# Splitting the last four weight chunks of a two-layer transformer kernel by token tile

## The chip, the cores and the metric

The kernel runs on one core of a Trainium2 chip. The metric is the device time of one launch, in microseconds. Three runs of the kernel before gave 2450.44, 2450.83 and 2454.04 us; the median is 2450.83 us. The engines are TensorE (PE, with PEld for its weight loads), VectorE (DVE), ScalarE (ACT), GpSimd (POOL) and SyncE (SP), whose queue issues nearly all the transfers.

## The reference

Two transformer layers run one after the other on 256 tokens of width 2048 in float32. What matters here is the end of the second one:

```
h = h + (silu(hn @ w_gate) * (hn @ w_up)) @ w_down      # w_down: 5632 x 2048
out = h * rsqrt(mean(h*h, axis=-1) + 1e-6) * final_norm  # one mean for each token
```

The mean is taken over all 2048 columns of a token, so no element of `out` can be scaled before the last column of the token's `h` is known. Two tokens never depend on each other in these two lines.

## The kernel before

Tokens lie on the 128 partitions, in two token tiles `t = 0, 1` (`NT`). Every large product is a list of groups, and each group yields 512 output columns (`CW`) for both tiles in two PSUM banks, `acc[g][0]` and `acc[g][1]`. The weights of a group come in chunks of 256 rows (`KC` = 2 times 128) by 512 columns, 512 KB each, through a ring of four slots (`RING`). SyncE loads a chunk into `w_raw` (L384), ACT rounds it to `w_hi` (L894), DVE forms the rest `w_lo` (L1206), and TensorE multiplies it (`columns`, L526 on). For each 128 rows and each tile there are three matmuls of 512 columns, high by high, high by low, low by high (L533 to L535), so 12 for a chunk. A slot is free for the next split when TensorE has used its chunk: each chunk's last matmul raises `w_used`, ACT waits on it for the chunk that comes four later, DVE waits for ACT, and TensorE for DVE (`w_split_lo`).

What each engine does beside this stream is listed by `plan()`: `put(n, step)` attaches a step to chunk `n`, and every engine runs its part of the steps between its chunks, in the order of the list. For each group of a down projection `residual` puts `res` (DVE adds the accumulators to the residual `x`, L1353), `square` (ACT squares the new columns and adds them up into `sumsq`, L1029), and in the second layer `times_gain` (DVE multiplies 512 columns of each tile by the final gain `fgain`, L1386) for the first three column groups. The second layer's down projection has four groups of 22 chunks. After the fourth comes `rstd`: DVE reduces the four partial sums of both tiles and adds epsilon (L1357, L1359), and POOL raises the result to the power -0.5 (L442).

Then the output is normalised. DVE takes columns 0 to 1023 and 1024 to 1535 of tile 0 (L1538) and columns 1536 to 2047 of both tiles, these with the gain (L1540); ACT takes columns 0 to 1535 of tile 1 in two parts (L1185). SyncE stores the output in four transfers of 128 x 1024 (L419), and waits for them.

Of the kernel before, what the change touches and what calls it, by code (L numbers as in the profile page):

```python
# [9 lines left out]
ALU = mybir.AluOpType  # L10
ACT = mybir.ActivationFunctionType
# [42 lines left out]
def plan():  # L54
# [10 lines left out]
    def put(n, *step):  # L65
        at.setdefault(n, []).append(step)
# [32 lines left out]
    def residual(n, g, b, gain):  # L99
        put(b, "res", g, n)  # L100
        put(b + 1, "square", g, n)
        if gain is not None:
            put(b + 1, "turn_x", n, g)
            put(b + 2, "split_x", n, gain, 0)
            put(b + 3, "split_x", n, gain, 1)
        elif n < 3:
            put(b + 3, "times_gain", n)
        if n == 3:
            put(b + (3 if gain is not None else 1), "rstd")


    for n in range(4):
# [80 lines left out]
        b = group("w_up_2", CW * j, CW, whole, "x")  # L193
    for n in range(4):
        b = group("w_down_2", CW * n, CW, list(range(FT // KC)), "f")
        residual(n, len(groups) - 1, b, None)
    return groups, first, at, up1, up2, b


# [19 lines left out]
def two_layer_kernel(nc, a, out):  # L219
# [6 lines left out]
    with ctx:  # L226
# [22 lines left out]
        hsum, hmean, hrstd = sb("hsum", [P, NT, 4]), sb("hmean", [P, NT, 4]), sb("hrstd", [P, NT, 4])  # L249
        lsum, lmean = sb("lsum", [P, 2, NT]), sb("lmean", [P, 2, NT])  # L250
        lrstd = sb("lrstd", [P, 2, NT])
        negmax, psum_, pinv = sb("negmax", [P, 4]), sb("p_sum", [P, 4]), sb("p_inv", [P, 4])

        with ExitStack() as r:
# [43 lines left out]
        pbuf = half_a.rearrange("p a b -> p (a b)")[:, 0:2 * KEYS]  # L298
        pT = half_b.rearrange("p a b -> p (a b)")[:, 0:2 * KEYS]
        rel = half_a.rearrange("p a b -> p (a b)")  # L300
        fgain = halves[:].rearrange("p s a b -> p (s a b)")

        acc = [[ctx.enter_context(nc.psum_tensor(f"acc{g}{t}", [P, CW], F32)) for t in range(NT)] for g in range(2)]
# [11 lines left out]
        gqk_ready, premultiplied, angles, tables = sem("gqk_ready"), sem("premultiplied"), sem("angles"), sem("tables")  # L315
# [9 lines left out]
        hidden, hidden_hi, f_ready = sem("hidden"), sem("hidden_hi"), sem("f_ready")  # L325
        dve_step, pool_step, normalised = sem("dve_step"), sem("pool_step"), sem("normalised")
        normalised_act = sem("normalised_act")

        block = ctx.enter_context(nc.Block())

# [30 lines left out]
        @block.sync  # L361
        def _(sp):
            chunk = Count()

            def load_x(n):

                sp.dma_start(x[:, :, n * CW:(n + 1) * CW],
                             a["x"][0].rearrange("(t p) d -> p t d", p=P)[:, :, n * CW:(n + 1) * CW]).then_inc(x_loaded[n], 16)

            def load(name, col, width, c):  # L370
                if chunk.now >= RING:

# [12 lines left out]
                chunk.now += 1  # L385

            def pair(j, wa, ca, wb, cb):
                for w, c0 in ((wa, ca), (wb, cb)):
                    for c in range(KT // KC):
                        load(w, j * CW + c0, CW, c)  # L390

            sp.dma_start(ident[:], a["c_ident"]).then_inc(ident_loaded, 16)
            sp.dma_start(rows[0:G_ROWS, 0:P], a["gains"]).then_inc(rows_loaded, 16)
            g = 0
            while g < len(groups):
                if g == G_UP1:
                    with_loop(sp, {"chunk": chunk}, lambda j: pair(j, "w_up", 0, "w_up", DFF), {"chunk": 16})
                    g += 2 * PAIRS
                elif g == G_UP2:
                    with_loop(sp, {"chunk": chunk}, lambda j: pair(j, "w_gate_2", 0, "w_up_2", 0), {"chunk": 16})  # L400
                    g += 2 * PAIRS
                else:
                    name, col, width, ks, _ = groups[g]
                    for c in ks:
                        if chunk.now < 4:
                            load_x(chunk.now)
                        load(name, col, width, c)
                        if name == "w_down_2" and col == 0 and c == 16:

                            sp.dma_start(fgain, a["final_norm_2"].rearrange("(a n) -> a n", a=1).to_broadcast([P, D]))\  # L410
                              .then_inc(fgain_loaded, 16)
                    g += 1

            for t, h, by_vector, by_scalar in ((0, 0, 1, 0), (1, 0, 0, 1), (0, 1, 3, 0), (1, 1, 4, 2)):
                if by_vector:
                    sp.wait_ge(normalised, by_vector)
                if by_scalar:
                    sp.wait_ge(normalised_act, by_scalar)
                sp.dma_start(out[0, t * P:(t + 1) * P, h * 2 * CW:(h + 1) * 2 * CW],  # L419
                             x[:, t, h * 2 * CW:(h + 1) * 2 * CW]).then_inc(stored, 16)  # L420
            sp.wait_ge(stored, 16 * 2 * NT)

        @block.gpsimd
        def _(pool):
# [77 lines left out]
            for n in range(n_end + 8):  # L502
                for step_, *args in at.get(n, []):
                    if step_ == "isc" and args[0] == 5:

                        pool.wait_ge(rel_full, 6)
                        pool.dma_start(pool_w[:], a["pool_w"].rearrange("w (k p) d -> p w k d", p=P)).then_inc(pool_loaded, 16)
                    if step_ in mine:
                        mine[step_](*args)

        @block.tensor
        def _(pe):
# [13 lines left out]
            def columns(c, k, width, operand, start, stop, g):  # L526

                hi, lo = operand
                slot = chunk.now % RING
                for t in range(NT):  # L530
                    o = acc[g][t][:, 0:width]
                    l, m = hi[:, t * P:(t + 1) * P], lo[:, t * P:(t + 1) * P]
                    pe.matmul(o, l, w_hi[:, slot, k, 0:width], start=start, stop=False)  # L533
                    pe.matmul(o, l, w_lo[:, slot, k, 0:width], start=False, stop=False)  # L534
                    last = pe.matmul(o, m, w_hi[:, slot, k, 0:width], start=False, stop=stop)  # L535
                return last

            def kw_columns(c, g):
# [342 lines left out]
        def _(act):  # L881
# [296 lines left out]
                g += 1  # L1178
            for n in range(n_end - LEAD, n_end + 8):
                run(n)  # L1180
            act.wait_ge(rstd_ready, 5)
            act.wait_ge(premultiplied, 6)
            for lo_, hi_ in ((0, 2 * CW), (2 * CW, 3 * CW)):
                v = x[:, 1, lo_:hi_]
                act.activation(v, v, ACT.Copy, scale=rstd[:, 1:2]).then_inc(normalised_act, 1)  # L1185

        @block.vector
        def _(dve):
# [191 lines left out]
            def on_times_gain(n):  # L1380

                dve.wait_ge(squared, n_squared[0] + 2 * (n + 1))
                dve.wait_ge(fgain_loaded, 16)
                for t in range(NT):
                    v = x[:, t, n * CW:(n + 1) * CW]
                    dve.tensor_tensor(v, v, fgain[:, n * CW:(n + 1) * CW], ALU.mult).then_inc(premultiplied, 1)  # L1386

            def on_rstd():
                n_squared[0] += 8
# [34 lines left out]
            def run(n):  # L1424
                for step_, *args in at.get(n, []):
                    if step_ in mine:
                        mine[step_](*args)

            dve.memset(minus_half[:], -0.5).then_inc(consts_set, 1)
            dve.wait_ge(cols_ready, 1)  # L1430
            for m in range(KT // 2):
# [98 lines left out]
                run(n)  # L1530


            dve.wait_ge(rstd_ready, 5)
            dve.wait_ge(premultiplied, 6)
            for t, lo_, hi_ in ((0, 0, 2 * CW), (0, 2 * CW, 3 * CW), (0, 3 * CW, D), (1, 3 * CW, D)):
                v, r = x[:, t, lo_:hi_], rstd[:, t:t + 1]
                if hi_ < D:
                    dve.tensor_scalar(v, v, r, None, ALU.mult).then_inc(normalised, 1)  # L1538
                else:
                    dve.scalar_tensor_tensor(v, v, r, fgain[:, lo_:hi_], ALU.mult, ALU.mult).then_inc(normalised, 1)  # L1540


_WHOLE = ["x", "w_in", "pool_w", "w_out", "w_up", "w_down", "positions_2", "final_norm_2"]
# [38 lines left out]
```

## Time and profile before

| | us |
|---|---|
| median of 3 runs | 2450.83 |
| lowest, highest run | 2450.44, 2454.04 |
| span of the profiled execution | 2451.8 |
| PE busy | 2431.2 (99% of the span) |
| DVE busy | 1319.7 (54%) |
| ACT busy | 1181.0 (48%) |
| POOL busy | 55.8 (2%) |

For the profiled execution the page gives its span, from the first instruction to the last, and no time of its own beyond that. The span lies 1.0 us above the median of the three runs and inside their spread. PE is busy nearly all the time, and its granted clock is full over all 40 slices; only the last microseconds of the span have no matmul in them.

### The profile page before, as it was taken

The numbers are of one execution on the slowest core, as the hardware profiler recorded it, in microseconds if no ns is written. First come the engines' busy times: TensorE is split into PE (matmuls) and PEld (weight loads), VectorE is DVE, ScalarE is ACT, GpSimd is POOL, SyncE is SP. The second block draws the span as 40 slices with busy tenths as digits, with TensorE's granted clock in tenths as the row PEclk, the third lists the DMA queues.
The fourth block names the chain that finished last, engine by engine and source line by source line (L and its number), as shares of the span: only waits on it lengthen the run. The fifth ranks groups of instructions, "written<-read, shape, count | busy, mean of one in ns | idle before, by whom it ended". The sixth has DMA issues, their size and how long they took to land.

```text
span 2451.8 us, 29803 instructions
## 1 busy us (share of the span) xinstructions
PE 2431.2 (99%) x11143; PEld 2016.1 (82%) x11143; DVE 1319.7 (54%) x1478; ACT 1181.0 (48%) x1488; POOL 55.8 (2%) x96
## 2 busy tenths in 40 slices
PE   8999999999999999999999999999999999999998
PEld 7788888888888888888888888888888888888886
DVE  4675455666666655445454454565545445454443
ACT  5544455555555544445455544544444444444443
POOL 0000000000000000001120000000000000000000
PEclk9999999999999999999999999999999999999999
DMA  6565455555555555556655555555665666655653
GB/s 229 171 189 164 146 182 188 186 183 187 186 184 184 188 185 188 189 189 186 185 170 172 159 161 186 185 185 184 188 190 187 190 192 187 190 189 205 191 192 142
DMA packets 240899, 449.38 MB, mean 183 GB/s; under 512 B 20027, under 2 KB 26747, under 8 KB 240683
## 3 DMA queue, kind: packets, MB, share of 16 engines
q1 hardware_dynamic: 239904, 445.94, 57.4%
q0 software_dynamic: 544, 2.06, 0.3%
q8 instruction: 59, 0.97, 0.2%
q14 instruction: 29, 0.24, 0.0%
q10 hardware_dynamic: 363, 0.18, 0.0%
HBM read 446.02 MB, written 2.10 MB: 183 GB/s over the span
## 4 chain that ended last, share of the span: by engine, by line
PE 69%; issue 29%; DVE 0%; DMA 0%; ACT 0%; SPq 0%; POOLq 0%; POOL 0%; DVEq 0%; ACTq 0%
PE acc L533 22%; PE acc L535 22%; PE acc L534 21%; PE bank L524 2%; PE bank L665 1%; PE bank L693 0%; PE bank L723 0%; PE bank L642 0%; DMA x_res<-in_x 0%; PE bank L694 0%; PE bank L668 0%; DVE xT_lo L1321 0%; DVE w_lo L1206 0%; PE bank L708 0%; PE acc L545 0%
## 5 line engine op out<-in xcount | busy, mean ns | idle before, releaser
L1206 DVE TENSOR_TENSOR w_lo<-w_raw,w_hi 128x1024 fp32r<-128x1024 f32 (+1 forms) x844 | 1031.2, 1222 | 1084.5 <-ACT w_hi L894 1082.7
L894 ACT ACTIVATE w_hi<-w_raw 128x1024 fp32r<-128x1024 f32 (+1 forms) x844 | 891.1, 1056 | 1222.7 <-PE acc L535 1220.0
L533 PE MATMUL acc<-w_hi,xT_hi 128*128 128x512 f32 (+1 forms) x2240 | 881.1, 393 | 1.2 <-DVE w_lo L1206 1.2
L535 PE MATMUL acc<-w_hi,xT_lo 128*128 128x512 f32 (+1 forms) x2240 | 871.1, 389 | 0.0
L534 PE MATMUL acc<-w_lo,xT_hi 128*128 128x512 f32 (+1 forms) x2240 | 870.2, 388 | 0.0
L535 PEld LDWEIGHTS acc<-w_hi,xT_lo 128*128 128x128 f32 x2240 | 421.0, 188 | 87.6
L533 PEld LDWEIGHTS acc<-w_hi,xT_hi 128*128 128x128 f32 x2240 | 421.1, 188 | 87.3 <-issue 3.3
L534 PEld LDWEIGHTS acc<-w_lo,xT_hi 128*128 128x128 f32 x2240 | 421.4, 188 | 83.7
L533 PE MATMUL acc<-w_hi,f_hi 128*128 128x512 f32 x704 | 277.2, 394 | 0.0
L535 PE MATMUL acc<-w_hi,f_lo 128*128 128x512 f32 x704 | 276.1, 392 | 0.0
L534 PE MATMUL acc<-w_lo,f_hi 128*128 128x512 f32 x704 | 273.6, 389 | 0.0
L535 PEld LDWEIGHTS acc<-w_hi,f_lo 128*128 128x128 f32 x704 | 132.2, 188 | 30.3
L534 PEld LDWEIGHTS acc<-w_lo,f_hi 128*128 128x128 f32 x704 | 132.2, 188 | 29.5
L533 PEld LDWEIGHTS acc<-w_hi,f_hi 128*128 128x128 f32 x704 | 132.3, 188 | 26.6
L533 PE MATMUL acc<-w_hi,y_hi 128*128 128x512 f32 x256 | 101.1, 395 | 0.0
L535 PE MATMUL acc<-w_hi,y_lo 128*128 128x512 f32 x256 | 100.2, 391 | 0.0
L534 PE MATMUL acc<-w_lo,y_hi 128*128 128x512 f32 x256 | 100.1, 391 | 0.0
L1446 DVE SCALAR_TENSOR_TENSOR halves<-bank,cols,halves 128x254 f32<-128x254 f32 (+1 forms) x176 | 76.5, 476 | 5.9
L524 PE MATMUL bank<-ident,stage 128*128 128x128 f32 (+1 forms) x435 | 57.0, 272 | 4.4 <-DMA stage<-in_gains 4.4
L524 PEld LDWEIGHTS bank<-ident,stage 128*128 128x128 f32 (+1 forms) x435 | 50.9, 140 | 11.8 <-DMA stage<-in_gains 4.4
L535 PEld LDWEIGHTS acc<-w_hi,y_lo 128*128 128x128 f32 x256 | 48.1, 188 | 10.7
L534 PEld LDWEIGHTS acc<-w_lo,y_hi 128*128 128x128 f32 x256 | 48.1, 188 | 10.2
(189 smaller groups left out, 1162.9 us busy)
## 6 DMA issues: line engine op xcount, KB each, us to landing
w_raw<-in_w_up SPq DMA_DIRECT2D x264, 512.0 KB, 3.4
w_raw<-in_w_in SPq DMA_DIRECT2D x200, 512.0 KB, 3.6
w_raw<-in_w_down SPq DMA_DIRECT2D x176, 512.0 KB, 3.7
w_raw<-in_w_gate SPq DMA_DIRECT2D x88, 512.0 KB, 3.5
w_raw<-in_w_out SPq DMA_DIRECT2D x64, 512.0 KB, 3.6
w_raw<-in_w_branch_a SPq DMA_DIRECT2D x16, 512.0 KB, 3.5
w_raw<-in_w_branch_b SPq DMA_DIRECT2D x16, 512.0 KB, 3.6
w_raw<-in_w_in SPq DMA_DIRECT2D x10, 320.0 KB, 3.1
```

Of the source, the lines that this page charges most:

```text
L524: return pe.transpose(T[bank][:, pos:pos + part], src, ident[0:part, 0:part])
L533: pe.matmul(o, l, w_hi[:, slot, k, 0:width], start=start, stop=False)
L534: pe.matmul(o, l, w_lo[:, slot, k, 0:width], start=False, stop=False)
L535: last = pe.matmul(o, m, w_hi[:, slot, k, 0:width], start=False, stop=stop)
L665: last = pe.matmul(o, q[:, blk * P:(blk + 1) * P], k[:, 0:nk], start=True, stop=which != "mla")
L894: act.activation(in_slot(w_hi, slot, width), in_slot(w_raw, slot, width), ACT.Copy).then_inc(w_split_hi, 1)
L1206: dve.tensor_tensor(in_slot(w_lo, slot, width), in_slot(w_raw, slot, width), in_slot(w_hi, slot, width).bitcast(F32), ALU.subtract).then_i ...
L1446: last = dve.scalar_tensor_tensor(o, T[bank][:, cc * S:(cc + 1) * S - back], cols[:, bass.ds(j * 4 + k, 1)], o, ALU.mult, ALU.add)
```

## The change

TensorE goes through all but the last four chunks of the last group as before. Then it takes these four chunks for tile 0 alone (24 matmuls into `acc[..][0]`, `first_tile_done`), and after that the same four chunks for tile 1 (24 matmuls into `acc[..][1]`), raising `w_used` once for each chunk in this second pass. The steps `res`, `square` and `rstd` of the fourth column group leave the plan. In their place each tile has a sequence of its own at the end: DVE adds the accumulator to the residual in a separate buffer `last`, ACT squares and sums, POOL takes the power, DVE and ACT scale, and the tile is stored.

The sum over the first three column groups, with epsilon, is made earlier (`sum_before`), its square root (POOL) is put beside the 512 new columns as a 513th, and ACT's square-and-sum over 513 elements gives the whole sum in one instruction. The division by 2048 moves into the gain, which is multiplied once by sqrt(2048) in the step of the first column group. ACT's squares go to `spare` in SBUF, not to a PSUM bank. DVE normalises columns 0 to 1023 and 1536 to 2047 of each tile, ACT 1024 to 1535. Tile 0 is stored in two halves of 1024 columns by SyncE; tile 1 in columns 0 to 1023 and 1536 to 2047 by SyncE and 1024 to 1535 by ACT's own queue.

```diff
@@ plan @@
     for n in range(4):
         b = group("w_down_2", CW * n, CW, list(range(FT // KC)), "f")
-        residual(n, len(groups) - 1, b, None)
+        if n < 3:
+            residual(n, len(groups) - 1, b, None)
@@ sync @@
-            for t, h, by_vector, by_scalar in ((0, 0, 1, 0), (1, 0, 0, 1), (0, 1, 3, 0), (1, 1, 4, 2)):
...
+            sp.wait_ge(normalised, 1)
+            store(0, 0, 2 * CW)
+            sp.wait_ge(normalised, 2)
+            sp.wait_ge(normalised_act, 1)
+            store(0, 2 * CW, D)
+            sp.wait_ge(normalised, 3)
+            store(1, 0, 2 * CW)
+            sp.wait_ge(normalised, 4)
+            store(1, 3 * CW, D)
+            sp.wait_ge(stored, 16 * 5)
@@ gpsimd @@
+            pool.wait_ge(before_ready, 1)
+            for t in range(NT):
+                pool.tensor_tensor(last[:, t, CW:CW + 1], sum_before[:, t:t + 1], plus_half[:], ALU.pow).then_inc(root_ready, 1)
+            for t in range(NT):
+                pool.wait_ge(last_squared, t + 1)
+                pool.tensor_tensor(last_r[:, t:t + 1], sumsq[:, t, 3:4], minus_half[:, 0:1], ALU.pow).then_inc(last_rstd, 1)
@@ tensor @@
+            def last_columns(t, c, par, ends):
+
+                slot = (chunk.now + c) % RING
+                kt = (FT // KC - RING + c) * KC
+                for k in range(KC):
+                    h, l = f_hi[:, kt + k, t * P:(t + 1) * P], f_lo[:, kt + k, t * P:(t + 1) * P]
+                    pe.matmul(acc[par][t][:], h, w_hi[:, slot, k], start=False, stop=False)
+                    pe.matmul(acc[par][t][:], h, w_lo[:, slot, k], start=False, stop=False)
+                    last = pe.matmul(acc[par][t][:], l, w_hi[:, slot, k], start=False, stop=ends and k == KC - 1)
+                return last
...
-                for c, kc in enumerate(ks):
+                in_turn = ks[:-RING] if g == len(groups) - 1 else ks
+                for c, kc in enumerate(in_turn):
...
+                if g == len(groups) - 1:
+                    for c in range(RING):
+                        pe.wait_ge(w_split_lo, chunk.value(c + 1))
+                        last = last_columns(0, c, group.now % 2, c == RING - 1)
+                    last.then_inc(first_tile_done, 1)
+                    for c in range(RING):
+                        last_columns(1, c, group.now % 2, c == RING - 1).then_inc(w_used, 1)
+                    chunk.now += RING
@@ scalar @@
-            for lo_, hi_ in ((0, 2 * CW), (2 * CW, 3 * CW)):
-                v = x[:, 1, lo_:hi_]
-                act.activation(v, v, ACT.Copy, scale=rstd[:, 1:2]).then_inc(normalised_act, 1)
+            act.wait_ge(root_ready, 2)
+            for t in range(NT):
+                act.wait_ge(last_added, t + 1)
+                act.activation(spare[:, t, 0:CW + 1], last[:, t, 0:CW + 1], ACT.Square, accum_out=sumsq[:, t, 3:4]).then_inc(last_squared, 1)
+                act.wait_ge(last_rstd, t + 1)
+                v = x[:, t, 2 * CW:3 * CW]
+                act.activation(v, v, ACT.Copy, scale=last_r[:, t:t + 1]).then_inc(normalised_act, 1)
+            act.wait_ge(normalised_act, 2)
+            act.dma_start(out[0, P:2 * P, 2 * CW:3 * CW], x[:, 1, 2 * CW:3 * CW]).then_inc(stored, 16)
@@ vector @@
-                dve.wait_ge(fgain_loaded, 16)
+                if n == 0:
+                    dve.wait_ge(fgain_loaded, 16)
+                    link(dve.tensor_scalar(fgain, fgain, D ** 0.5, None, ALU.mult))
+                    linked()
...
+                if n == 2:
+                    link(dve.tensor_reduce(sum_before[:], sumsq[:, :, 0:3], AX.X, ALU.add))
+                    linked()
+                    dve.tensor_scalar(sum_before[:], sum_before[:], D * EPS, None, ALU.add).then_inc(before_ready, 1)
...
+            dve.memset(plus_half[:], 0.5)
...
-            for t, lo_, hi_ in ((0, 0, 2 * CW), (0, 2 * CW, 3 * CW), (0, 3 * CW, D), (1, 3 * CW, D)):
...
+            for t in range(NT):
+                if t == 0:
+                    dve.wait_ge(first_tile_done, 1)
                 else:
+                    finished(g_last)
+                v = x[:, t, 3 * CW:D]
+                dve.tensor_tensor(last[:, t, 0:CW], acc_last[t][:], v, ALU.add).then_inc(last_added, 1)
+                dve.wait_ge(last_added, t + 1)
+                link(dve.tensor_tensor(v, last[:, t, 0:CW], fgain[:, 3 * CW:D], ALU.mult))
+                dve.wait_ge(last_rstd, t + 1)
+                linked()
+                r = last_r[:, t:t + 1]
+                dve.tensor_scalar(x[:, t, 0:2 * CW], x[:, t, 0:2 * CW], r, None, ALU.mult).then_inc(normalised, 1)
+                dve.tensor_scalar(v, v, r, None, ALU.mult).then_inc(normalised, 1)
```

## Rows read from the trace of the kernel before

**Rows 1.** The page: span, busy time of the engines, and the chain's shares.
```profile
span 2451.8 us, 29803 instructions
...
PE 2431.2 (99%) x11143; PEld 2016.1 (82%) x11143; DVE 1319.7 (54%) x1478; ACT 1181.0 (48%) x1488; POOL 55.8 (2%) x96
...
PE 69%; issue 29%; DVE 0%; DMA 0%; ACT 0%; SPq 0%; POOLq 0%; POOL 0%; DVEq 0%; ACTq 0%
```

**Rows 2.** Timeline of PE at the last 49 matmuls: start, duration, what (us).
```profile
2429.41 0.39 PE L533 MATMUL acc<-w_hi,f_hi 128*128 128x512 f32 x1
2429.64 0.39 PE L534 MATMUL acc<-w_lo,f_hi 128*128 128x512 f32 x1
...
2439.94 0.39 PE L534 MATMUL acc<-w_lo,f_hi 128*128 128x512 f32 x1
2440.17 0.40 PE L535 MATMUL acc<-w_hi,f_lo 128*128 128x512 f32 x1
```

**Rows 3.** Timeline of ACT and DVE: the split of the last chunk.
```profile
2429.67 1.06 ACT L894 ACTIVATE w_hi<-w_raw 128x1024 fp32r<-128x1024 f32 x1 [1.69 <-PE acc L535]
...
2430.76 1.23 DVE L1206 TENSOR_TENSOR w_lo<-w_raw,w_hi 128x1024 fp32r<-128x1024 f32 x1 [1.52 <-ACT w_hi L894]
```

**Rows 4.** Timeline of DVE, ACT and POOL from the last matmul to the power.
```profile
2440.60 1.29 DVE L1353 TENSOR_TENSOR x_res<-acc,x_res 128x512 f32<-128x512 f32 x2 [8.62 <-PE acc L535]
...
2441.33 0.60 ACT L1029 ACTIVATE bank<-x_res 128x512 f32<-128x512 f32 x1 [10.60 <-DVE x_res L1353]
2441.86 0.18 ACT L1029 ACTIVATION_READ_ACCUMULATOR bank<-x_res 128x1 f32 x1
...
2442.68 0.19 ACT L1029 ACTIVATION_READ_ACCUMULATOR bank<-x_res 128x1 f32 x1
2442.90 0.16 DVE L1357 TENSOR_REDUCE meansq<-sumsq 128x2 f32<-128x8 f32 x1 [1.00 <-ACT bank L1029]
2443.09 0.17 DVE L1359 TENSOR_SCALAR meansq<-meansq 128x2 f32<-128x2 f32 x1
2443.34 0.70 POOL L442 TENSOR_TENSOR rstd<-meansq,minus_half 128x2 f32<-128x2 f32 x1 [720.77 <-DVE meansq L1359]
```

**Rows 5.** Timeline of DVE, ACT and SP: normalisation and stores.
```profile
2444.07 1.15 DVE L1538 TENSOR_SCALAR x_res<-x_res,rstd 128x1024 f32<-128x1024 f32 x2 [0.81 <-POOL rstd L442]
2444.85 0.36 SPq L419 DMA_DIRECT2D out<-x_res  x1
...
2445.80 0.74 DVE L1540 SCALAR_TENSOR_TENSOR x_res<-x_res,rstd,halves 128x512 f32<-128x512 f32 x1
```

**Rows 6.** Groups by line and shape on the residual: count, min/median/max in ns.
```profile
L1029 ACT ACTIVATE halves<-x_res x32: 612/631/642, 25.0 to 1713.8; 128x512 f32<-128x512 f32 x32
...
L1353 DVE TENSOR_TENSOR x_res<-acc,x_res x32: 680/682/692, 305.9 to 2441.2; 128x512 f32<-128x512 f32 x32
...
L1386 DVE TENSOR_TENSOR x_res<-x_res,halves x6: 682/684/687, 2269.8 to 2391.3; 128x512 f32<-128x512 f32 x6
...
L419 SPq DMA_DIRECT2D out<-x_res x4: 364/526/1108, 2444.9 to 2446.6; - x4
L1185 ACT ACTIVATE x_res<-x_res,rstd x2: 705/926/1147, 2444.1 to 2445.1; 128x1024 f32<-128x1024 f32 x1, 128x512 f32<-128x512 f32 x1
L1538 DVE TENSOR_SCALAR x_res<-x_res,rstd x2: 481/616/752, 2444.1 to 2444.7; 128x1024 f32<-128x1024 f32 x1, 128x512 f32<-128x512 f32 x1
```

**Rows 7.** POOL's powers by line and shape: count, busy us, mean ns, idle before.
```profile
L448 POOL TENSOR_TENSOR hrstd<-hmean,minus_half 128x8 f32<-128x8 f32 x4 | 10.2, 2548 | 145.5 <-DVE hmean L1234 145.5
...
L442 POOL TENSOR_TENSOR rstd<-meansq,minus_half 128x2 f32<-128x2 f32 x5 | 3.6, 712 | 2065.8 <-DVE meansq L1359 2065.7
...
L459 POOL TENSOR_TENSOR lrstd<-lmean,minus_half 128x2 f32<-128x2 f32 x2 | 1.9, 954 | 18.7 <-DVE lmean L1396 18.7
```

**Rows 8.** Transfers from 2440 to 2453: GB/s in 40 slices of 0.325 us.
```profile
GB/s 0 0 0 0 0 0 0 0 0 25 0 0 25 0 0 0 0 189 403 391 416 391 416 391 403 403 416 391 416 391 416 429 391 202 0 0 0 0 0 0
```

**Rows 9.** The line of the stores: time from issue to landing.
```profile
DMA to landing us min/median/max: 2.7/3.9/4.8
```

**Rows 10.** Transfers from 2350 to 2440: packets and rate; then the queue's share.
```profile
DMA packets 7407, 14.31 MB, mean 159 GB/s; under 512 B 440, under 2 KB 440, under 8 KB 7404
...
q1 hardware_dynamic: 7404, 14.26, 46.5%
```

**Rows 11.** Timeline of DVE around the first `times_gain`.
```profile
2269.85 1.29 DVE L1386 TENSOR_TENSOR x_res<-x_res,halves 128x512 f32<-128x512 f32 x2
2271.46 1.23 DVE L1206 TENSOR_TENSOR w_lo<-w_raw,w_hi 128x1024 fp32r<-128x1024 f32 x1 [0.32 <-ACT w_hi L894]
```

More of the change, by code:

```diff
@@ L105, in residual @@
             put(b + 3, "split_x", n, gain, 1)
-        elif n < 3:
+        else:
             put(b + 3, "times_gain", n)
         if n == 3:
-            put(b + (3 if gain is not None else 1), "rstd")
+            put(b + 3, "rstd")
     for n in range(4):
@@ L251, in two_layer_kernel @@
         lrstd = sb("lrstd", [P, 2, NT])
+        sum_before, last_r, plus_half = sb("sum_before", [P, NT]), sb("last_r", [P, NT]), sb("plus_half", [P, 1])
         negmax, psum_, pinv = sb("negmax", [P, 4]), sb("p_sum", [P, 4]), sb("p_inv", [P, 4])
@@ L300, in two_layer_kernel @@
         rel = half_a.rearrange("p a b -> p (a b)")
+        last = stage[:].rearrange("p g t c -> p g (t c)")
+        spare = w_raw[:].rearrange("p r k n -> p r (k n)")
         fgain = halves[:].rearrange("p s a b -> p (s a b)")
@@ L314, in two_layer_kernel @@
         kw_turned, kw_scaled = sem("kw_turned"), sem("kw_scaled")
-        gqk_ready, premultiplied, angles, tables = sem("gqk_ready"), sem("premultiplied"), sem("angles"), sem("tables")
+        gqk_ready, angles, tables = sem("gqk_ready"), sem("angles"), sem("tables")
         consts_set, squared, mean_ready, rstd_ready = sem("consts_set"), sem("squared"), sem("mean_ready"), sem("rstd_ready")
@@ L327, in two_layer_kernel @@
         normalised_act = sem("normalised_act")
+        first_tile_done, last_added, last_squared, last_rstd, before_ready, root_ready = (sem(n) for n in (
+            "first_tile_done", "last_added", "last_squared", "last_rstd", "before_ready", "root_ready"))
         block = ctx.enter_context(nc.Block())
@@ L412, in _, with store @@
                     g += 1
-            for t, h, by_vector, by_scalar in ((0, 0, 1, 0), (1, 0, 0, 1), (0, 1, 3, 0), (1, 1, 4, 2)):
[L415 to L421, printed above, removed]
+            def store(t, lo_, hi_):
+                sp.dma_start(out[0, t * P:(t + 1) * P, lo_:hi_], x[:, t, lo_:hi_]).then_inc(stored, 16)
+            sp.wait_ge(normalised, 1)
[8 more added lines that the diff above has]
+            sp.wait_ge(stored, 16 * 5)
         @block.gpsimd
@@ L1180, in _ @@
                 run(n)
-            act.wait_ge(rstd_ready, 5)
-            act.wait_ge(premultiplied, 6)
-            for lo_, hi_ in ((0, 2 * CW), (2 * CW, 3 * CW)):
-                v = x[:, 1, lo_:hi_]
-                act.activation(v, v, ACT.Copy, scale=rstd[:, 1:2]).then_inc(normalised_act, 1)
+            act.wait_ge(root_ready, 2)
[7 more added lines that the diff above has]
+            act.dma_start(out[0, P:2 * P, 2 * CW:3 * CW], x[:, 1, 2 * CW:3 * CW]).then_inc(stored, 16)
         @block.vector
@@ L1382, in on_times_gain @@
                 dve.wait_ge(squared, n_squared[0] + 2 * (n + 1))
-                dve.wait_ge(fgain_loaded, 16)
+                if n == 0:
+                    dve.wait_ge(fgain_loaded, 16)
+                    link(dve.tensor_scalar(fgain, fgain, D ** 0.5, None, ALU.mult))
+                    linked()
                 for t in range(NT):
                     v = x[:, t, n * CW:(n + 1) * CW]
-                    dve.tensor_tensor(v, v, fgain[:, n * CW:(n + 1) * CW], ALU.mult).then_inc(premultiplied, 1)
+                    link(dve.tensor_tensor(v, v, fgain[:, n * CW:(n + 1) * CW], ALU.mult))
+                if n == 2:
+                    link(dve.tensor_reduce(sum_before[:], sumsq[:, :, 0:3], AX.X, ALU.add))
+                    linked()
+                    dve.tensor_scalar(sum_before[:], sum_before[:], D * EPS, None, ALU.add).then_inc(before_ready, 1)
             def on_rstd():
@@ L1530, in _ @@
                 run(n)
-            dve.wait_ge(rstd_ready, 5)
-            dve.wait_ge(premultiplied, 6)
-            for t, lo_, hi_ in ((0, 0, 2 * CW), (0, 2 * CW, 3 * CW), (0, 3 * CW, D), (1, 3 * CW, D)):
-                v, r = x[:, t, lo_:hi_], rstd[:, t:t + 1]
-                if hi_ < D:
-                    dve.tensor_scalar(v, v, r, None, ALU.mult).then_inc(normalised, 1)
-                else:
-                    dve.scalar_tensor_tensor(v, v, r, fgain[:, lo_:hi_], ALU.mult, ALU.mult).then_inc(normalised, 1)
+            g_last = len(groups) - 1
+            acc_last = acc[g_last % 2]
+            for t in range(NT):
+                if t == 0:
+                    dve.wait_ge(first_tile_done, 1)
+                else:
+                    finished(g_last)
[8 more added lines that the diff above has]
+                dve.tensor_scalar(v, v, r, None, ALU.mult).then_inc(normalised, 1)
 _WHOLE = ["x", "w_in", "pool_w", "w_out", "w_up", "w_down", "positions_2", "final_norm_2"]
```

## The prediction

> **What bounds the kernel now.** I read the page first. PE is busy for 2431.2 of 2451.8 us and the chain that ended last is matmuls and their issue; the other engines are busy half the time or less [rows 1]. So nearly all the time is matmuls, one after the other, and the change removes none. The timeline of PE at the end shows their pace: starts at 2429.41 and 2440.17 with 47 steps between them, 10.76 / 47 = 0.229 us for one matmul of 512 columns, 2.75 us for a chunk of 12 [rows 2]. The last one ends at 2440.57, and 2451.8 - 2440.57 = 11.2 us have no matmul. Only this tail can change, so I followed the end engine by engine.
>
> The tail has two parts with different limits. In the first, one engine waits for another. DVE adds tile 0 and tile 1 (from 2440.60), ACT squares both (last read ends at 2442.68 + 0.19), DVE reduces and adds epsilon (to 2443.26), POOL takes the power (2443.34 to 2444.04) [rows 4]; the first 1024 columns are scaled from 2444.07 on, and SyncE issues the first store at 2444.85 [rows 5]. In the second part the transfers rule. The rate stands near 403 GB/s from the middle of slice 18 to the middle of slice 34, each 0.325 us long, so from 2445.7 to 2450.9: 5.2 us, and 4 x 524,288 bytes / 5.2 us = 403 GB/s [rows 8]. The last data are ready at 2445.80 + 0.74 = 2446.54 [rows 5], long before. So the end is set by the start of the first store and by the bytes that follow it, not by the normalisation that ends last. From the last packet to the end of the span it is 0.9 us.
>
> **The change, part by part.**
>
> *Matmuls.* Their number stays (48 for the last four chunks), and tile 1's last should still end at 2440.57. The first of the 48 starts at 2429.41; tile 0's 24th starts 23 x 0.229 later, at 2434.68, and ends at 2435.08 [rows 2]. The order costs nothing if the weights are ready. The pass over tile 0 takes the chunks at twice the pace: the fourth is wanted at its 19th matmul, 2429.41 + 18 x 0.229 = 2433.5. Its split waits for the chunk ahead of these four to be used, as before: ACT from 2429.67, DVE from 2430.76 to 2431.99 [rows 3], 1.5 us ahead. The third is wanted at 2432.2 and split a chunk earlier than the fourth, at 2429.2. Cost 0; if this cover were gone, all lateness would come through. That the four slots are released later is waited for by nothing, since no load follows.
>
> 24 matmuls in a row into one bank don't stand in the trace; three in a row do, and the step inside such a three is the same 0.23 us as the mean over all [rows 2]. I bound the cost from 0 to rival B and take 0, the end that the pace inside the threes is nearest to.
>
> *Tile 0's own end*, from 2435.1: add 0.68, to 2435.8 [rows 6]; square and read 0.72, to 2436.6 [rows 4]; POOL 0.41 (below) with hops, to 2437.1; DVE 0.75 + 0.48, to 2438.4, with ACT's 0.71 beside it [rows 6]. Its stores are issued at 2437.9 and 2438.4, start moving 0.85 us later (before: 2444.85 to 2445.7 [rows 5, 8]), and take 2.6 us for 1 MB: out by 2441.4. All of it lies beside tile 1's matmuls, and DVE is free 2.2 us before it is wanted at 2440.60. Cost 0; 1 MB of stores leaves the tail.
>
> *Tile 1's own end.* Add from 2440.60. ACT started at 2441.33 on the first add alone, and so it will now, to 2441.86 + 0.18 = 2442.04 [rows 4]. Its squares go to SBUF: 0.631 us there against 0.602, 0.03 more [rows 4, 6]; a 513th column is 1/512 of that. DVE's product with the gain (0.68 [rows 6]) runs beside ACT, over by 2442.0. POOL starts 0.08 us after its input, as it did behind DVE [rows 4]. Its power took 2.548 us over 8 columns and 0.712 over 2 [rows 7], so (2.548 - 0.712) / 6 = 0.31 a column and 0.10 fixed, an estimate of 0.41 for one column. Bounds: 0.41, and the 0.95 of the slower two-column power [rows 7]; I take 0.41. So POOL ends at 2442.55, DVE scales 1024 columns in 0.75 [rows 6] from 2442.58 to 2443.33, and the store is issued at 2443.35 against 2444.85: 1.5 us earlier. Of this 0.83 is the second square (between the ends of the two reads), 0.39 the reduction and epsilon (2442.87 to 2443.26) [rows 4], 0.3 POOL.
>
> ACT's 512 columns are done at 2442.58 + 0.71 = 2443.3 and are issued on its own queue; DVE's last 512 at 2443.33 + 0.48 = 2443.8 [rows 6]. SyncE's first issue takes 0.36 us [rows 5], so the second isn't held up. An issue by ACT behind data isn't in the rows; by SyncE's four it costs 0.36 to 1.11 us [rows 6], and at either the packets are queued before the first 512 KB are out. Cost 0.
>
> *The stores.* Packets start at 2443.35 + 0.85 = 2444.2. The 1,048,576 bytes in the tail need 2.6 us at 403 GB/s [rows 8]. Half of them now have rows of 2 KB in place of 4 KB. The weight loads have 2 KB rows: 159 GB/s at a share of 46.5% is 342 GB/s at full share [rows 10], 1.5 us for the half against 1.3. So 2.6 to 2.8 us, I take 2.7: last packet at 2446.9 and, with the same 0.9 us behind it, the end at 2447.8. It was 2451.8: **4.0 us less**, 1.5 from the chain and 2.5 from the transfers. Bounds: 4.1 with the faster rate; 3.6 with the slower rate for all bytes (3.1 us), and 3.1 with the slower power too.
>
> Does the last store alone end later than the backlog? The first of before landed in 2.7 us with 1.3 of moving [rows 9], so 1.4 are fixed; 256 KB issued at 2443.8 would land at 2443.8 + 1.4 + 0.65 = 2445.9. The backlog is later.
>
> The stores of this trace ran at 403 GB/s for 5 us [rows 8]. The Trainium skill ("DMA: Bandwidth & Descriptors", Specifications) gives about 358 GB/s as one core's limit to HBM. By it the 1 MB would take 2.9 us and the saving would be 3.8; the trace disagrees, and the measurement decides.
>
> *Earlier edits.* Scaling the gain adds one DVE instruction over 2048 columns. From 0.481 us for 512 and 0.752 for 1024 [rows 6] each further 512 costs 0.27, so about 1.3 us. It stands ahead of a split that started at 2271.46; the products before it ended at 2271.14 [rows 11], now at about 2272.5, so this split comes 1.1 us late. A split ends 2.3 us after ACT starts it [rows 3], and the ring gives it three chunks, 8.2 us: 5.8 us of slack hide it. The reduction and addition into `sum_before` (0.16 + 0.17 [rows 4]) are hidden likewise, two root instructions run on an idle POOL, and the new memset stands ahead of waits for the first transfers. Cost 0; without cover 1.3 + 0.4 us.
>
> **The sum.** The span goes from 2451.8 to 2447.8. The median of before is 1.0 us below its profiled span; I take the 4.0 off the median: 2450.8 - 4.0 = **2446.8 us**, 0.16% less. A measurement of this kernel tells 0.2%, 4.9 us, from no change, so this counts as no change unless it reaches 2445.9.
>
> **The rivals.**
>
> *A: the transfers stop being the limit.* If the stores of two queues drain faster than those of one, the last landing sets the end: 2445.9 + 0.4 = 2446.3, which is 5.5 less, 2445.3 us. For it: the last store waits for nothing else. Against: one queue already kept the rate steady near 403 GB/s, slice after slice [rows 8]. With the scatter of medians added, 16% that the time passes the 4.9 us.
>
> *B: one bank for 24 matmuls is slower.* If a matmul into the same bank had to see the one before it finish, the pace would be its 0.39 us instead of 0.229 [rows 2], 48 x 0.16 = 7.7 us more, less 4.0: +3.7, 2454.5 us, slower than before. The step at which it decides is 4.0 / 48 = 0.08 us a matmul; with 0.19 more it passes 2455.7. Against it: the pace inside the present threes. 4%.
>
> *C: a handover is late.* DVE comes late to tile 1 if tile 0's end takes over 5.5 us; the split's 1.5 us are used up; or POOL's power on one column is no shorter than 0.95. Each costs 0.5 to 3 us: 2447.3 to 2449.8. For it: five hops a tile, and POOL's spans are rough. Against it: 1.5 to 2.2 us of room in the first two. 13%.
>
> *D: it doesn't do what it says*: the four stores still bunch at the end, 2450.8 us. Tile 0's would have to come 5 us late for that. 2%.
>
> **How the numbers follow.** The forecast with a saving of 3.1 to 4.8: 65%; A 16, B 4, C 13, D 2. The medians scatter by about 1 us (two runs 0.4 apart, one at 2454.04). The range takes the forecast with that scatter, A down to 2445.1 and most of C: 2445.1 to 2449.5. Faster than 2445.9: 16%; slower than 2455.7: 3%, B at its worst or a disturbed median; 81% within.
>
> **What would show it.** In the profile after: PE keeps 0.229 us through the last 48 with no wait for `w_lo`; DVE's adds start near 2435.1 and 2440.6; POOL's last power takes 0.41 us and ends near 2442.55; tile 1's first store is issued near 2443.35; the rate line shows two humps of 2.7 us, the first over by 2441.5, the second from 2444.2 to 2446.9; span near 2447.8. It is wrong if PE shows gaps in the last 11 us, if tile 0's stores reach into the tail, or if the last hump is much longer than 2.8 us.

## The result

The changed kernel takes 2463.24 us (median of 5 runs, 2461.76 to 2464.69) against 2451.48 (5 runs, 2450.44 to 2454.04): the ratio is 1.0047, 95% interval 1.0036 to 1.0058. It is 11.8 us slower. The forecast was 2446.8, 4 us faster, within 2445.1 to 2449.5, with a chance of 3% for slower by more than 0.2%: the direction is wrong and the time is far outside the range.

The page of the changed kernel, span and busy time:

```profile
span 2462.2 us, 29808 instructions
...
PE 2445.3 (99%) x11143; PEld 2016.1 (82%) x11143; DVE 1321.7 (54%) x1482; ACT 1181.0 (48%) x1488; POOL 57.8 (2%) x99
```

Against [rows 1] the span grew by 10.4 us and PE's busy time by 14.1, with the same 11143 matmuls. So PE lost 14.1 us and 3.7 were gained elsewhere. The busy times of DVE, ACT and POOL changed by 2.0 us or less.

**Where the 14 us are.** The timeline of PE, one row at each end of 24 matmuls (8 rows of this line apart); the columns are start and modelled duration. First products of `x` (up projection, near 700 us), then of `f` (last down projection). The kernel before:

```profile
699.76 0.39 PE L533 MATMUL acc<-w_hi,xT_hi 128*128 128x512 f32 x1
...
705.20 0.39 PE L533 MATMUL acc<-w_hi,xT_hi 128*128 128x512 f32 x1
...
2299.63 0.39 PE L533 MATMUL acc<-w_hi,f_hi 128*128 128x512 f32 x1
...
2305.12 0.39 PE L533 MATMUL acc<-w_hi,f_hi 128*128 128x512 f32 x1
```

The changed kernel:

```profile
700.00 0.39 PE L551 MATMUL acc<-w_hi,xT_hi 128*128 128x512 f32 x1
...
705.44 0.39 PE L551 MATMUL acc<-w_hi,xT_hi 128*128 128x512 f32 x1
...
2299.75 0.40 PE L551 MATMUL acc<-w_hi,f_hi 128*128 128x512 f32 x1
...
2305.35 0.40 PE L551 MATMUL acc<-w_hi,f_hi 128*128 128x512 f32 x1
```

The step, the time from one matmul's start to the next one's, is the difference of two such rows divided by 24. `x` steps at 5.44 / 24 = 0.2267 us in both. `f` stepped at 5.49 / 24 = 0.2288 and now steps at 5.60 / 24 = 0.2333. The same holds at 300 us, in products of `y`, and at 1650, in those of `m_hl`: places whose instructions the change doesn't touch. 3384 matmuls have a stationary operand other than `x` (2112 `f`, 768 `y`, 384 `m_hl`, 120 latents); 3384 x 0.0045 = 15 us, the 14.1 of the page. The granted clock is 1.00 in both.

What `y`, `m_hl`, the latents and `f` have in common, and `x` has not, is their place in SBUF. The change allocates three small tensors (`sum_before`, `last_r`, `plus_half`) behind `minus_half` and the other small ones. Counted as 32 bytes a partition each, they move all that is allocated later by 96 bytes. `x` and the weights' buffers are allocated earlier and stay.

**The tail** did nearly as forecast. ACT, DVE, POOL and the queues of the changed kernel at tile 1's end, in that order:

```profile
2455.38 0.63 ACT L1222 ACTIVATE w_raw<-stage 128x513 f32<-128x513 f32 x1 [3.44 <-DVE stage L1591]
2455.91 0.19 ACT L1222 ACTIVATION_READ_ACCUMULATOR w_raw<-stage 128x1 f32 x1
...
2457.51 0.39 ACTq L1227 DMA_DIRECT2D out<-x_res  x1
```

```profile
2449.05 0.69 DVE L1591 TENSOR_TENSOR stage<-acc,x_res 128x512 f32<-128x512 f32 x1 [3.22 <-PE acc L564]
...
2454.65 0.69 DVE L1591 TENSOR_TENSOR stage<-acc,x_res 128x512 f32<-128x512 f32 x1 [2.29 <-PE acc L564]
...
2456.76 0.75 DVE L1597 TENSOR_SCALAR x_res<-x_res,last_r 128x1024 f32<-128x1024 f32 x1 [0.69 <-POOL last_r L527]
```

```profile
2456.18 0.54 POOL L527 TENSOR_TENSOR last_r<-sumsq,minus_half 128x1 f32<-128x1 f32 x1 [5.00 <-ACT w_raw L1222]
```

```profile
2457.54 0.81 SPq L422 DMA_DIRECT2D out<-x_res  x2
```

The last matmul ends at 2454.62 (2454.22 + 0.40). From there to the end of the span it is 7.6 us; it was 11.2 [rows 1, 2]. SyncE issues tile 1's first store 2.92 us after the last matmul, where it was 4.28 [rows 5]. DVE was free for tile 1 in time: it waited 2.29 us for tile 1's last matmul.

The transfers of the changed kernel from 2450 to 2462.2, GB/s in 40 slices of 0.305 us:

```profile
GB/s 0 0 0 27 0 27 0 0 0 295 416 349 430 416 416 389 403 322 0 0 0 0 0 0 0 0 0 255 416 389 369 383 423 349 383 389 81 0 0 0
```

There are two humps in place of the one of [rows 8]. Tile 0's ends at 2455.4; tile 1's lasts from 2458.4 to 2461.0, 2.7 us in place of 5.2.

### The profile page after: what moved, and what is told of

It reads as the page before. It is cut to its first block, busy times and chain, and to the rows that moved or that the text cites. A ratio compares the mean times of both kernels' runs of the same rounds, so it can differ in the third digit from the quotient of the medians.

```text
span 2462.2 us, 29808 instructions
## 1 busy us (share of the span) xinstructions
PE 2445.3 (99%) x11143; PEld 2016.1 (82%) x11143; DVE 1321.7 (54%) x1482; ACT 1181.0 (48%) x1488; POOL 57.8 (2%) x99
## 4 chain that ended last, share of the span: by engine, by line
PE 99%; DVE 0%; DMA 0%; issue 0%; ACT 0%; SPq 0%; POOLq 0%; POOL 0%; DVEq 0%; ACTq 0%
PE acc L551 31%; PE acc L553 31%; PE acc L552 31%; PE bank L542 3%; PE bank L703 1%; PE bank L731 0%; PE bank L761 0%; PE bank L680 0%; DMA x_res<-in_x 0%; PE bank L732 0%; PE bank L706 0%; PE bank L746 0%; DVE xT_lo L1363 0%; DVE w_lo L1248 0%; PE acc L564 0%
```

## The experiments

Places below are byte offsets in a partition, counted through the kernel's allocations in their order, each start on a multiple of 32. No trace shows an address. What speaks for the count is that experiments three and six, 64 bytes added before the change and 96 + 224 after it, come to the same distance by it and have the same step, where 16 bytes off cost the step in nearly every group of experiment ten. "Distance" is the start of the stationary operand less the start of the weights' buffer it is multiplied with, modulo 256 (the parts used later lie at multiples of 512 from these starts). I began with another idea, that a start on a multiple of 64 is what counts; two experiments overturned it and its successor.

### One: the changed kernel, 32 bytes of padding

```diff
-negmax, psum_, pinv = sb("negmax", [P, 4]), sb("p_sum", [P, 4]), sb("p_inv", [P, 4])
+negmax, psum_, pinv = sb("negmax", [P, 4]), sb("p_sum", [P, 4]), sb("p_inv", [P, 4]); sb("pad", [P, 8])
```

> The changed kernel with one unused tensor of 32 bytes a partition behind the small tensors, ahead of y_hi; nothing else differs. The three new small tensors take 96 bytes there, so that all large tensors behind them (y_hi, y_lo, m_hl, f_hi, f_lo, cqT) begin at 32 past a multiple of 64, where before they began on one. Theory P (position): the matmuls whose stationary operand lies there step at 0.2333 us in place of 0.2288, which is the loss; with the pad the step is 0.2288 again in all groups, PE busy falls from 2445.3 to about 2431, and the time is that of before less the shorter tail (11.2 us before, 7.6 in the changed kernel): 2451.5 - 3.6 = 2447.9 us. Theory C (code): another layout of the instructions or the added semaphores slow PE; the pad changes nothing and the time stays at 2463.

Measured: 2462.86 us (ratio 1.0048, 1.0034 to 1.0062), `f` at 0.2333. A multiple of 64 doesn't do it. By this run alone theory C stood as well.

### Two: the kernel before, 32 bytes

```diff
+; sb("pad", [P, 8])
```

> The kernel before with the same unused 32 bytes, and no other edit. Theory P: y, m and f products step at 0.2333 us, PE busy rises by about 14 us, time 2451.5 + 14 = 2465.5 us, with not one instruction changed. Theory C: nothing moves, 2451.5.

Measured: 2466.2 us (1.0062, 1.0048 to 1.0076). Its page, and `f` in the timeline of PE:

```profile
span 2464.4 us, 29803 instructions
...
PE 2445.1 (99%) x11143; PEld 2014.5 (82%) x11143; DVE 1319.5 (54%) x1478; ACT 1181.8 (48%) x1488; POOL 55.7 (2%) x96
```

```profile
2299.71 0.39 PE L533 MATMUL acc<-w_hi,f_hi 128*128 128x512 f32 x1
...
2305.31 0.39 PE L533 MATMUL acc<-w_hi,f_hi 128*128 128x512 f32 x1
```

PE's busy time rises by 13.9 us with not one instruction changed (29803 in both). An unused tensor is enough for the whole loss. That the change's instructions add nothing to it is shown by experiment six.

### Three: the kernel before, 64 bytes

```diff
+; sb("pad", [P, 16])
```

> The kernel before with 64 unused bytes: the large tensors move but begin again on a multiple of 64 (now of 128 too). Theory P in the form that only the place within 64 bytes counts: 2451.5 us, same steps. Rival: any shift against the weights' buffers slows it (then about 2465), or a multiple of 128 is better still (then under 2449, with a step below 0.2288 in the y, m and f products).

Measured: 2445.67 us (0.9975, 0.9965 to 0.9986), 6 us faster than the kernel before. The rival was right that there is something better:

```profile
span 2443.5 us, 29803 instructions
...
PE 2423.9 (99%) x11143; PEld 2017.1 (83%) x11143; DVE 1319.5 (54%) x1478; ACT 1180.9 (48%) x1488; POOL 55.7 (2%) x96
```

```profile
2300.17 0.39 PE L533 MATMUL acc<-w_hi,f_hi 128*128 128x512 f32 x1
...
2305.61 0.39 PE L533 MATMUL acc<-w_hi,f_hi 128*128 128x512 f32 x1
```

`f` is at 5.44 / 24 = 0.2267, as `x` is in all kernels up to here. The kernel before was itself at a middle level.

### Four: the old order of the last four chunks

In the kernel of experiment one:

```diff
                     for c in range(RING):
                         pe.wait_ge(w_split_lo, chunk.value(c + 1))
                         last = last_columns(0, c, group.now % 2, c == RING - 1)
-                    last.then_inc(first_tile_done, 1)
-                    for c in range(RING):
+                        if c == RING - 1:
+                            last.then_inc(first_tile_done, 1)
                         last_columns(1, c, group.now % 2, c == RING - 1).then_inc(w_used, 1)
```

> The changed kernel with the pad of 32 bytes and the last four chunks in the old order: each chunk for tile 0, then for tile 1; the two tiles' ends keep their new sequences, tile 0's starting when its last matmul is done, now 6 matmuls (1.4 us) before the end in place of 24 (5.5 us). If the order by tiles is what takes 1 MB of stores out of the tail: tile 0's stores are issued about 2.8 us after its last matmul, so some 1.4 us behind PE's end, DVE comes to tile 1 only after tile 0's scaling, at about PE's end + 2.1 us, and the span ends 2.5 to 3.5 us later than the padded kernel: 2450.5 to 2451.5 us. Rival: the gain of the tail is all from the shorter chain (one square, no reduction), and the order is worth under 1 us: 2448.0 to 2449.0.

Measured: 2465.84 us against 2462.86 of experiment one on the same chip, 3.0 us more; the runs of the two just overlap (2464.60 to 2465.92 against 2462.37 to 2465.21). (The absolute times were expected with the padding's gain, which didn't come; the difference is what counts.) In the profiled executions the tail is 9.4 us against 7.6. DVE comes to tile 1 late:

```profile
2454.20 0.75 DVE L1597 TENSOR_SCALAR x_res<-x_res,last_r 128x1024 f32<-128x1024 f32 x1 [0.74 <-POOL last_r L527]
2454.87 0.48 DVE L1598 TENSOR_SCALAR x_res<-x_res,last_r 128x512 f32<-128x512 f32 x1
2455.27 0.68 DVE L1591 TENSOR_TENSOR stage<-acc,x_res 128x512 f32<-128x512 f32 x1
```

The last matmul ended at 2453.41, DVE adds tile 1 at 2455.27. So the order by tiles is worth 2 to 3 us, and it costs PE nothing: both kernels step at 0.2333 in this group, two passes or one.

### Five and six: the changed kernel, 96 and 224 bytes

```diff
+; sb("pad", [P, 24])      # experiment six: [P, 56]
```

> The changed kernel with 96 unused bytes ahead of y_hi, so that y, m and f begin on a multiple of 128 (of 256 too, 0 within 512 bytes counted as 256). So far the step of the products was: 0.2267 us where the stationary operand began at 128 within 512 (x in all kernels; y, m, f in the padded kernel before), 0.2288 at 64, 0.2333 at 96, 160 and 192. Theory M128 (a multiple of 128 is what counts): 0.2267 in all groups, PE busy about 2424, time 2445.7 less the 3.6 us of the shorter tail: 2442 us, faster than both. Theory M256 or relative (only the same place within 256 or 512 bytes as the weights' buffer, which is at 128): step 0.2288 or 0.2333, 2447.9 to 2462.

> The changed kernel with 224 unused bytes: y, m, f begin at 384 within 512 bytes, 128 within 256. M128: as with 96 bytes, 2442 us. M256: 0.2267 here and not there. Only the same place within 512 as before (128): slow in both.

Measured: 2459.9 us (1.0033, 1.0022 to 1.0043) with 96 and **2440.98 us** (0.9955, 0.9938 to 0.9972) with 224. The page and PE's timeline with 224:

```profile
span 2438.8 us, 29808 instructions
...
PE 2423.0 (99%) x11143; PEld 2015.3 (83%) x11143; DVE 1322.0 (54%) x1482; ACT 1180.6 (48%) x1488; POOL 58.2 (2%) x99
```

```profile
2299.82 0.39 PE L551 MATMUL acc<-w_hi,f_hi 128*128 128x512 f32 x1
...
2305.26 0.39 PE L551 MATMUL acc<-w_hi,f_hi 128*128 128x512 f32 x1
```

A multiple of 128 isn't enough (96 bytes: 0.2325), the same place within 256 is (0.2267). PE's busy time is 2423.0 us, against 2423.9 in experiment three, which has the old instructions at the same distance: the change's instructions, the two passes among them, cost PE nothing. The changed kernel so placed beats the kernel before by 10.7 us and experiment three by 4.7. What is left open is whether the place counts by itself or against the weights' buffers.

### Seven and eight: moving x, moving the weights' buffers

```diff
 # seven
-xT_hi, xT_lo = sb("xT_hi", ...), sb("xT_lo", ...)
+sb("pad_a", [P, 8]); xT_hi, xT_lo = sb("xT_hi", ...), sb("xT_lo", ...); sb("pad_b", [P, 8])
 # eight
-w_hi, w_lo = sb("w_hi", ...), sb("w_lo", ...)
+sb("pad_a", [P, 8]); w_hi, w_lo = sb("w_hi", ...), sb("w_lo", ...); sb("pad_b", [P, 8])
```

> The kernel before with 32 unused bytes ahead of xT_hi and 32 behind xT_lo: x begins at 160 within 512 bytes, the weights' buffers at 192, y, m and f at 128. If only the stationary operand's own place counts: x products (6720 matmuls) step at 0.2333 for 0.2267, 44 us more; the other 3384 at 0.2267 for 0.2288, 7 us less; 2451.5 + 37 = 2489 us. If its place relative to the weights' buffer counts: x at -32 is slow (+44), y, m, f at -64 stay at 0.2288, as in the kernel before (also -64): 2496 us. If the weights' own place counts, the y, m and f products go to 0.2333: 2511 us.

> The kernel before with 32 unused bytes ahead of w_hi and 32 behind w_lo: w_hi and w_lo begin at 160 within 512 bytes, x, y, m and f at 128. If only the stationary operand's place counts: all products at 0.2267, 2445.7 us (as the kernel before with 64 bytes). If the moving operand's place counts, alone or relative to the stationary one (now -32): all products at about 0.2333, 10104 matmuls x 0.0066 = 67 us over 2445.7: 2512 us.

Measured: seven 2491.9 us (1.0161, 1.0135 to 1.0187), eight 2506.6 us (1.0222, 1.0195 to 1.0248). The total of seven doesn't decide, 2489 and 2496 are both near; the steps do. PE's timeline in seven, `x` then `f`:

```profile
700.17 0.39 PE L533 MATMUL acc<-w_hi,xT_hi 128*128 128x512 f32 x1
...
705.77 0.39 PE L533 MATMUL acc<-w_hi,xT_hi 128*128 128x512 f32 x1
...
2299.81 0.39 PE L533 MATMUL acc<-w_hi,f_hi 128*128 128x512 f32 x1
...
2305.30 0.39 PE L533 MATMUL acc<-w_hi,f_hi 128*128 128x512 f32 x1
```

`x` is at 0.2333 now. `f` begins at 128 within 256, the place that gave 0.2267 in three and six, but steps at 0.2288 here, since the buffers moved by 64: the distance is -64, as in the kernel before. In eight only the buffers are moved, and the products of `x`, `y`, `m_hl` and `f` all step at 0.2333. PE's busy time in eight:

```profile
PE 2485.3 (99%) x11143; PEld 2013.0 (80%) x11143; DVE 1319.4 (53%) x1478; ACT 1182.1 (47%) x1488; POOL 54.6 (2%) x96
```

### Nine: everything off by 32

```diff
+sb("pad_a", [P, 8])  # ahead of xT_hi; and sb("pad_b", [P, 16]) ahead of y_hi
```

> The kernel before with 32 unused bytes ahead of xT_hi, so that every large tensor moves by 32, and 64 more ahead of y_hi. x, the weights' buffers, y, m and f then all begin at 160 within 512 bytes: none on a multiple of 64, and all at distance 0 from each other within 256. Theory R (the distance of the stationary operand from the weights' buffers, counted within 256 bytes, sets the step: 0 gives 0.2267 us, -64 0.2288, -32, +32, +64 and +128 0.2325 to 0.2334): every product at 0.2267, 2445.7 us, as the kernel before with 64 bytes. Theory A (the place of either operand by itself counts): all products at 0.233, about 2507 to 2512 us.

Measured: 2444.7 us (0.9971, 0.9960 to 0.9983), within the intervals the same as experiment three. PE's busy time and timeline:

```profile
PE 2423.3 (99%) x11143; PEld 2015.0 (82%) x11143; DVE 1319.6 (54%) x1478; ACT 1181.0 (48%) x1488; POOL 55.7 (2%) x96
```

```profile
2300.09 0.39 PE L533 MATMUL acc<-w_hi,f_hi 128*128 128x512 f32 x1
...
2305.53 0.39 PE L533 MATMUL acc<-w_hi,f_hi 128*128 128x512 f32 x1
```

By the count no large tensor begins on a multiple of 64, and all products have the fast step. Against experiment three a shift of everything by 32 changed nothing, and a shift of the buffers alone by 32 cost 62 us: it is the distance between stationary operand and weights' buffer that counts, not the place of either.

### Ten: two more distances

```diff
+; sb("pad", [P, 16])               # as in experiment three
+sb("pad_y", [P, 40], F32, r)      # ahead of y_hi
-f_hi, f_lo = sb("f_hi", [P, FT, S], F32R, r), sb("f_lo", [P, FT, S], F32R, r)
+f_raw = sb("f_raw", [P, 2 * FT * S + 4], F32R, r)
+f_hi = f_raw[:, 4:4 + FT * S].rearrange("p (a b) -> p a b", b=S)
+f_lo = f_raw[:, 4 + FT * S:4 + 2 * FT * S].rearrange("p (a b) -> p a b", b=S)
```

> The kernel before with 64 unused bytes (all distances 0), and then f moved by 16 bytes and y, m and the latents by 160. It measures two further distances of theory R: f at +16 (2112 matmuls), y, m and latents at +160 (1272), x still at 0. If any distance other than 0 and -64 costs the full step of 0.2333: 3384 x 0.0066 = 22 us over 2445.7, 2468 us. If 16 bytes are too little to matter, f stays at 0.2267 and the time is about 2454. If +160 = -96 is between, y and m at 0.229 to 0.233.

Measured: 2464.76 us (1.0054, 1.0039 to 1.0070). `f`, 16 bytes off, steps at 0.2333 in seven of its eight groups, and so do `y` and `m_hl` at +160. So 16 bytes can cost the full step. But the third group of the first down projection, from 995 to 1056 us, has the fast step from end to end. PE's timeline in the first group, then in the third:

```profile
890.15 0.39 PE L536 MATMUL acc<-w_hi,f_raw 128*128 128x512 f32 x1
...
895.75 0.39 PE L536 MATMUL acc<-w_hi,f_raw 128*128 128x512 f32 x1
...
1010.64 0.39 PE L536 MATMUL acc<-w_hi,f_raw 128*128 128x512 f32 x1
...
1016.08 0.39 PE L536 MATMUL acc<-w_hi,f_raw 128*128 128x512 f32 x1
```

That is 5.60 / 24 = 0.2333 and 5.44 / 24 = 0.2267. The two groups have the same `f`, and by the kernel's counters the same ring slots and the same PSUM banks. So where the distance isn't 0, the addresses alone don't fix the step; what else does isn't known.

### Eleven: tile 0's stores held back

In the kernel of experiment six:

```diff
-            sp.wait_ge(normalised, 1)
+            sp.wait_ge(normalised, 3)
             store(0, 0, 2 * CW)
```

> The changed kernel with 224 unused bytes (2441.0 us), and SyncE waiting for tile 1's first normalised columns before it issues tile 0's stores: all 2 MB of stores lie in the tail again, the rest of the change stays. The forecast put 2.5 us of its 4.0 on the megabyte that leaves the tail. If that term is right: 2443.5 us, and the last hump of the stores lasts 5.2 us in place of 2.7. Rival: the order's 3 us (the padded kernels with and without it: 2465.8 against 2462.9) come from DVE's and ACT's queues, not from the transfers; then under 1 us is lost here.

Measured: 2443.54 us (0.9965, 0.9951 to 0.9978), 2.6 us over experiment six; in the profiled executions the tail is 10.2 us against 7.6. The transfers from 2425 to 2441.9, GB/s in 40 slices of 0.42 us:

```profile
GB/s 0 0 0 0 0 0 0 19 0 19 0 0 0 0 0 0 0 0 0 0 0 0 0 0 87 427 397 368 417 407 397 397 427 388 407 359 397 87 0 0
```

One hump of 5.2 us again. Only SyncE's first wait differs, so the transfers alone cost this. The forecast's term of 2.5 us for the megabyte that leaves the tail is right.

### Twelve: only w_lo off

```diff
-w_hi, w_lo = sb("w_hi", ...), sb("w_lo", ...)
+w_hi = sb("w_hi", ...); sb("pad_a", [P, 8]); w_lo = sb("w_lo", ...); sb("pad_b", [P, 8])
```

> The kernel before with 32 unused bytes between w_hi and w_lo and 32 behind w_lo: x, y, m and f are at distance 0 from w_hi and at -32 from w_lo. It asks which matmuls pay. If a matmul pays by the distance of the operands that are read while it streams, then only the third that stream w_lo (3368 of 10104) step at 0.2333, the other two thirds stay at 0.2267: 3368 x 0.0066 = 22 us over 2445 us, 2467 us, and in the timeline one start-to-start step in three is longer. If all pay once one of the buffers is off: 2507 to 2512 us. If none pays as long as w_hi is at 0: 2445 us.

Measured: 2495.2 us (1.0180, 1.0163 to 1.0197), between the theories: of the 62 us of PE's busy time that moving both buffers costs (2485.3 against 2423.3 in nine), `w_lo` alone brings 49.9 (2473.2). `f` steps at 0.2311 in the first layer and at 0.2333 in the second; in the first layer's up projection of `x` one group of 512 columns steps at 0.2311, the next at 0.2333, and so on. PE's timeline in two groups, one after the other:

```profile
671.56 0.39 PE L533 MATMUL acc<-w_hi,xT_hi 128*128 128x512 f32 x1
...
677.11 0.39 PE L533 MATMUL acc<-w_hi,xT_hi 128*128 128x512 f32 x1
...
693.34 0.40 PE L533 MATMUL acc<-w_hi,xT_hi 128*128 128x512 f32 x1
...
698.93 0.40 PE L533 MATMUL acc<-w_hi,xT_hi 128*128 128x512 f32 x1
```

The step behind a matmul that streams `w_lo` is the longest, 0.236 to 0.237 on the mean for `x`, `y`, `m_hl` and `f`. Those behind the other two are 0.231 and 0.226 for `f` in the first layer and both 0.232 in the second. So more matmuls pay than the third that stream `w_lo`, and not the same ones everywhere. Why isn't settled.

All steps together, as the median over stretches of 24 matmuls (us; the distances are those from `w_hi`):

```
distance          0       -64      -32      +16      +32      +64     +128     +160
step           0.2267   0.2288   0.2333   0.2333   0.2333   0.2333   0.2325   0.2333
seen in        x of the  y m f    f of 2,  f of 10  y m f    y m f    y m f    y m of 10
               two kern., of be-  x of 7,           of the   of 1, 4  of 5
               3 6 9 11  fore, 7  all of 8          changed
```

Three runs leave this table in single groups: in experiment five one group of the first down projection (933 to 995 us) stepped at 0.2333, in ten one at 0.2267, and in twelve groups alternate. In the other runs the steps of `x`, `y`, `m_hl` and `f` are those of the table in every group.

## Why the prediction was wrong

1. **The failed step is the first: "tile 1's last should still end at 2440.57", at cost 0.** It ended at 2454.62. I took PE's pace as given by the matmuls' number and shape, and priced the change's instructions, waits and transfers, but not its allocations. The three new tensors moved `y`, `m_hl` and `f` from distance -64 to +32, worth +14.1 us of PE's time. The trace of the kernel before held a hint that I didn't take up: I worked out 0.229 us for `f` and never compared it with the pace of `x`, which is 0.2267 for the same shape. Two paces for one instruction mean that something beside the instruction sets it.
2. **Rival B** named slower matmuls, but others and by another cause: 0.16 us more for each of the last 48, 3.7 us over the kernel before in all. The two passes cost nothing: the last 48 step at 0.2333 like the rest of `f`, and at 0.2267 in experiment six. A loss of 0.0045 us on 3384 matmuls decided, and the time was 11.8 us over. No rival named it.
3. **The weights' cover** held: no wait of PE for `w_lo` was added. The last split ended at 2445.83, and the 19th matmul of tile 0's pass, which needs it, was due at 2443.25 + 18 x 0.2333 = 2447.45: 1.6 us ahead (forecast 1.5).
4. **Tile 0's end beside tile 1's matmuls**: right. DVE was 2.3 us early (forecast 2.2), and tile 0's stores were out 3 us before tile 1's began.
5. **Tile 1's chain**: 1.36 us shorter in place of 1.5. POOL's power over one column took 0.54 us, not 0.41; a straight line through two sizes was too low, and the bounds held it.
6. **The stores**: one megabyte in 2.7 us, as forecast, and experiment eleven gives 2.6 us for bringing the other one back (forecast 2.5). From the last packet to the end it was 1.2 us for 0.9.
7. **The sum of the tail**: 3.6 us against 4.0, so rival A didn't come about: with two queues the last megabyte still moved at 1,048,576 bytes / 2.7 us = 388 GB/s. (The 0.4 us that rival A adds behind the last landing stand in no row.) At equal steps the medians say the same: experiment one against two 2462.9 - 2466.2 = -3.3, six against three 2441.0 - 2445.7 = -4.7.
8. **The gain's scaling** took 1.22 us (forecast 1.3) and was hidden.

That the allocations cause the loss is shown by experiment two (nothing else changed) and six (nothing else added). That the distance counts, not the place, is shown by seven, eight and nine. Why a distance costs, why -64 costs 0.0021 us where most others cost 0.0066, and why single groups at the same addresses have another step, is open.

## What to carry to other kernels

Where matmuls fill the time, a new tensor of 32 bytes a partition ahead of an operand can cost more than a good edit gains (14.5 us in experiment two, against 3.6 us of the tail): write down the start of each matmul operand modulo 256 before and after an edit, and keep the difference between stationary and moving operand where it was, or try it at 0. Compare the start-to-start step of the same matmul shape across all its operands; if the steps differ, there is time to be had without touching an instruction (here 6 us from 64 unused bytes). When an edit of the tail is measured, compare the pace of the untouched part first: the tail's 3.6 us of gain were real and invisible under 14 us of loss.

## What the runs showed of the hardware

- The step of a 128 x 128 by 512 matmul in this float32 format took 0.2267, 0.2288 or 0.2325 to 0.2333 us at the same granted clock, 1.00, mostly by the distance modulo 256 bytes between stationary operand and weights' buffer (eight distances were tried): 2.9% between the ends, about 62 us of this kernel when all products are off (experiment eight against nine).
- The modelled duration of one matmul hardly shows it (0.39 against 0.40 us), and the weight loads show 0.187 to 0.188 us with all products off (experiment eight) as with none (nine). Only start-to-start steps do.
- Sixteen bytes of displacement cost as much as 32 in seven groups of eight, and nothing in the eighth (experiment ten). So the step is not a function of the addresses alone.
- POOL's power took 0.54 us over one column and 0.70 over two.
